# One slot between the turn of the attention weights and their product with the values, from tile 2 on

## The chip, the cores and the metric

The kernel runs on one core of a Trainium2 chip. The metric is the device time of one execution in microseconds, as a median of several runs. The core has five engines that run side by side, each through its own list of instructions in order: TensorE (matmul), VectorE, ScalarE, GpSimd and SyncE. They wait for one another through semaphores. Transfers between the main memory (HBM) and the on-chip memories run on 16 DMA engines; here SyncE issues the ordinary ones and GpSimd the gathers. TensorE writes its results to banks of a small memory (PSUM), from which VectorE and ScalarE read.

## The reference, cut to what matters

The program is one step of a one-layer decoder over 1024 prompt tokens and 32 sample tokens (8 sequences of 4, with 512 cached tokens each), width 1024, all in float32:

```python
x = x + concat(diff_attention(rmsnorm(x) @ W_in), pool_mixer(...)) @ W_out   # 4 heads, 4 pooling groups
x = x + peer(rmsnorm(x))            # 8 heads x 16 chosen experts a token, out of 16384
x = x + sigmoid(rmsnorm(x) @ W_gate) * (p @ W_ple)
y = rmsnorm(x)
# attention of one head: a = softmax(q1 k1 + bias) - lam * softmax(q2 k2 + bias);  out = a @ v
# peer: for each token and head, gather 16 rows u and 16 rows v from the tables;
#       out += sum_k gate_k * gelu(xn . u_k) * v_k
```

## The kernel before, in words

The prompt is cut into 8 tiles of 128 tokens. The peer part sets the beat of the whole program. For each tile and peer head, 16 rows of the joined table (a row of u and a row of v, 8 KB together) are gathered for each of the 128 tokens. One gather fetches one such row for all 128 tokens. The ring `uv_rows` holds 8 gathers. A *slot* is the work for two gathers; a peer head has 8 slots and a tile 64. There are 528 slots with the samples, numbered s = 0, 1, ..., and 19 more before them with negative numbers, which hold the first work of the program.

In slot s the engines do this. GpSimd (`fetch`) issues two gathers, each when the adds that used its place in the ring are done, so it fetches the rows of slot s + 4 when those of slot s have been added. VectorE (`dot`) takes the dot products of two gathered rows with the tokens, and after them a step of the choice of experts for a later peer head (`choose_part`). ScalarE (`weigh`) applies the gelu to the dots and writes two scaled diagonals, `diag`. TensorE (`add_rows`, lines 974 and 976) multiplies the diagonals by the v halves and so adds them to two banks. In every eighth slot (s = 2 modulo 8) TensorE also computes the scores of the experts for a later head (`route`, line 949).

All other work is laid over these slots. The order of each engine's instructions is written out by slot numbers: in every slot, each engine runs `front_step(s)`, which asks for each piece whether it belongs to s. TensorE runs it before `add_rows` of the same slot, ScalarE after `weigh`, VectorE after the dots and the step of the choice. Slots 0 to 63 project the tiles. Attention for tiles 0 and 1 is done before slot 0 and for tiles 2 to 7 in slots 67 to 189. Then the samples' attention follows, and from slot 322 the gates. `ATT[t]` holds the slots of a tile t:

- `turn`, `band`, `pool`: q and k are turned (line 553), then the pooling products (lines 589 and 591, then 601).
- `scores`: for each of the 4 heads the scores in one or two chunks (line 617). VectorE adds bias and takes the maxima (line 1532), and ScalarE takes the exponentials (line 1193), one slot later (`late`).
- `keys`: VectorE combines the two softmaxes to the weights of a head (line 1550).
- `weights`: TensorE turns the weights of a head to banks TA and TB (line 629), and ScalarE copies them to on-chip memory (`keep_weights`, lines 1203 and 1208).
- `values`: TensorE multiplies the turned weights by the values (line 648). Before it, it waits until the copy has emptied the banks. After the last head ScalarE copies the sums (`keep_values`).
- `norm`, `heads`, `out`: the norm over each head, the turn of the heads (line 553; VectorE copies it in the next slot, line 1584), and two halves of the output product, each 8 matmuls of 128x512 (line 671), which VectorE adds to x in the next slot (line 1592). SyncE loads and stores x around it.

The start of each tile from 2 on is a number written out in `attention_slots` (67, 84, 101, 123, 145, 167). Before the change, `values` from tile 2 on are the same slots as `weights`; for tiles 0 and 1 they are one slot later. `norm`, `heads` and `out` are reckoned from the last of them, `end`. In `front_step` of TensorE the pieces of one slot come in this order: for each tile turn, band, pool, heads, scores, output; then weights, then values. `BACK_FREE`, and from it every slot of the samples (`C0`, `C_PAGE`, `C_SCORES`, `C_VALUES`, `C_OUT`, `C_END`), is reckoned from the last output slot of tile 7. The gate jobs' slots are numbers written out.

Of the kernel before, what the change touches and what calls it, by code (L numbers as in the profile page):

```python
# [87 lines left out]
Attention = namedtuple("Attention", "load load_s1 turn band pool chunks scores keys weights values norm heads out")  # L88


def attention_slots(t):

    if t < EARLY:
        b = -LEAD + (1, 4)[t]
        first = -LEAD + (2, 6)[t]
        scores = [[first + h] for h in range(H)]
        weights = [first + 2 + h for h in range(H)]
        values = [first + 3 + h for h in range(H)]
        end = values[-1]
        return Attention(None, None, b, b + 1, b + 2, [(0, (t + 1) * T)], scores, weights, weights, values,  # L100
                         (end + 1, end + 1), end + 2, (end + 3, end + 4))
    b = {2: 67, 3: 84, 4: 101, 5: 123, 6: 145, 7: 167}[t]
    W = (t + 1) * T
    if W <= 512:
        chunks = [(0, W)]
        scores = [[b + 3 + 2 * h] for h in range(H)]
    else:
        cut = min(512, W - NEAR)
        chunks = [(0, cut), (cut, W)]
        scores = [[b + 3 + 3 * h, b + 4 + 3 * h] for h in range(H)]  # L110
    keys = [s[-1] + 2 for s in scores]
    weights = [s[-1] + 3 for s in scores]
    end = weights[-1]
    if t == EARLY:
        load = load_s1 = W_IN_FREE
    else:
        load, load_s1 = (ATT[t - 1].weights[h] + 1 for h in (H - 2, H - 1))
    return Attention(load, load_s1, b, b + 1, b + 2, chunks, scores, keys, weights, weights, (end + 1, end + 2), end + 3,
                     (end + 5, end + 6))


# [1 line left out]
for t in range(NT):  # L123
    ATT.append(attention_slots(t))
# [2330 lines left out]
```

## Time and profile before

| what | value |
|---|---|
| time, median of 3 runs | 3189.36 us (3188.24 to 3190.01) |
| the profiled execution, its own time | 3185.96 us |
| its span on the core | 3184.0 us |
| TensorE, VectorE, ScalarE, GpSimd busy | 74%, 70%, 30%, 41% |
| moved by DMA | 1266.57 MB, mean 398 GB/s over the span |
| slots with two gathers each | 528 (1056 gathers) |

The busy time of an engine says how much of the span it works. The profile's rows also name what an engine waited for: an arrow in brackets gives the idle time before an instruction and the engine and line that released it. The table of stretches shows the transfer rate beside the busy times, and the clock that TensorE was granted as a share of 2.4 GHz.

### The profile page before, as it was taken

To read this page: it belongs to the slowest core of one execution; us is meant where nothing else is said; L and a number is where in the kernel's file an instruction comes from. 1 tells how busy PE (TensorE), PEld (TensorE's weight loads), DVE (VectorE), ACT (ScalarE), POOL (GpSimd) and SP (SyncE) were. 2 spreads that over 40 slices of the span, in tenths; PEclk is the share of its full clock that TensorE was granted. 3 is DMA by queue.
4 is the path that set the end of the run, shared out by engine and by line. 5 is a ranking of instruction groups with operands and counts; after the bars stand their busy time and mean duration, and the time that the engine had idled before them with its cause. 6 is when DMAs were issued, how large, how long until landed. Compare 5 with 4: busy or idle time off the path is not lost.

```text
span 3184.0 us, 53323 instructions
## 1 busy us (share of the span) xinstructions
PE 2356.8 (74%) x20876; PEld 934.7 (29%) x20876; DVE 2234.2 (70%) x5466; ACT 950.0 (30%) x2427; POOL 1314.7 (41%) x1143
## 2 busy tenths in 40 slices
PE   8879999668777778757876667576777676677656
PEld 3543334223333333313432222122222222222112
DVE  1366667768778688756667666577777777777775
ACT  2212232234335354312322122123332322223222
POOL 0024433433334343435654543344444444444442
PEclk9999999878989889867788887788888897888778
DMA  6579999999999999999999999999999999999996
GB/s 264 179 284 420 421 413 417 417 416 395 416 417 409 407 416 416 412 409 418 417 416 411 417 416 410 414 410 416 407 414 417 420 407 421 408 420 410 420 416 281
DMA packets 202899, 1266.57 MB, mean 398 GB/s; under 512 B 24144, under 2 KB 27496, under 8 KB 60944
## 3 DMA queue, kind: packets, MB, share of 16 engines
q0 software_dynamic: 159808, 1133.76, 86.8%
q1 hardware_dynamic: 41404, 129.11, 10.2%
q8 instruction: 164, 2.69, 0.3%
q14 instruction: 87, 0.71, 0.1%
q10 hardware_dynamic: 1436, 0.29, 0.0%
HBM read 1234.61 MB, written 28.65 MB: 397 GB/s over the span
## 4 chain that ended last, share of the span: by engine, by line
DMA 31%; PE 14%; DVE 6%; POOL 3%; issue 3%; DVEq 2%; ACT 2%; POOLq 0%; ACTq 0%
DMA ring<-in_uv,idx 31%; PE sc L974 7%; DVE ring L1831 3%; POOL ring L2045 3%; PE sc L1007 2%; PE route L949 1%; DVEq L1841 1%; PE sc L976 1%; ACT diag L1367 1%; ACT hgelu L1362 0%; PE sc L873 0%; DVE x L1880 0%; PE sc L967 0%; PE sc L843 0%; POOL front L2061 0%
## 5 line engine op out<-in xcount | busy, mean ns | idle before, releaser
L2045 POOL DMA_INDIRECT ring<-in_uv,idx x1056 | 1235.2, 1170 | 1661.1 <-PE sc L976 1421.9
L974 PE MATMUL sc<-ring,diag 32*32 32x512 f32 x8192 | 1246.1, 728 | 667.6 <-ACT diag L1367 617.8
L1831 DVE CUSTOM_DVE_ANT_0 ring<-ring,xn_cur 128x1024 f32<-128x1024 f32 x1056 | 1280.2, 1221 | 652.8 <-DMA ring<-in_uv,idx 647.3
L976 PE MATMUL sc<-ring,diag 32*32 32x512 f32 x8192 | 1246.1, 728 | 0.0
L974 PEld LDWEIGHTS sc<-ring,diag 32*32 32x32 f32 x8192 | 273.1, 118 | 1456.0 <-ACT diag L1367 1033.1
L1362 ACT ACTIVATE hgelu<-hdot 128x2 f32<-128x2 f32 x528 | 107.5, 204 | 1816.4 <-DVE hdot L1831 1816.0
L1367 ACT ACTIVATE diag<-gate_d,hgelu 128x32 f32<-128x32 f32 x1056 | 281.8, 314 | 21.2
L976 PEld LDWEIGHTS sc<-ring,diag 32*32 32x32 f32 x8192 | 272.3, 118 | 2.3 <-issue 2.3
L531 PE MATMUL sc<-big,front 128*128 128x512 f32 x448 | 209.4, 612 | 3.6 <-DVE front L1477 3.5
L1362 ACT ACT_TABLE_LOAD x128 | 164.2, 1283 | 2.2
L949 PE MATMUL route<-big,xnT 128*128 128x256 f32 x560 | 135.3, 396 | 0.0
L949 PEld LDWEIGHTS route<-big,xnT 128*128 128x128 f32 x560 | 107.3, 197 | 52.3 <-issue 38.3
L949 PE MATMUL route<-front,xnT 128*128 128x256 f32 x464 | 111.9, 396 | 13.4 <-DMA front<-wqk_scratch 12.6
L531 PEld LDWEIGHTS sc<-big,front 128*128 128x128 f32 x448 | 83.0, 193 | 125.3 <-issue 124.8
L1007 PE MATMUL sc<-front 128*128 128x512 f32 x256 | 118.0, 604 | 0.0
L949 PEld LDWEIGHTS route<-front,xnT 128*128 128x128 f32 x464 | 88.9, 197 | 53.5 <-issue 27.9
L671 PE MATMUL sc<-big,front 128*128 128x512 f32 x192 | 87.2, 607 | 0.0
L1831 DVE DVE_READ_ACCUMULATOR2_ANT hdot<- 128x1 f32 x1056 | 86.5, 82 | 0.0
L648 PE MATMUL work<-big,front 128*128 128x128 f32 x264 | 41.1, 312 | 58.4 <-ACT front L1208 24.2
L1355 ACT ACT_TABLE_LOAD x65 | 83.4, 1283 | 1.1
L1007 PEld LDWEIGHTS sc<-front 128*128 128x128 f32 x256 | 46.3, 189 | 69.6 <-issue 69.4
L1193 ACT ACTIVATE front<-front 128x384 f32<-128x384 f32 (+5 forms) x48 | 41.9, 874 | 54.8 <-DVE front L1532 54.8
(296 smaller groups left out, 2311.0 us busy)
## 6 DMA issues: line engine op xcount, KB each, us to landing
front<-wqk_scratch SPq DMA_DIRECT2D x27, 1024.0 KB
ring<-in_uv,idx POOLq DMA_INDIRECT x1056
big<-in_w_in SPq DMA_DIRECT2D x8, 1024.0 KB, 14.3
wqk_scratch<-front SPq DMA_DIRECT2D x8, 1024.0 KB, 6.8
big<-wqk_scratch SPq DMA_DIRECT2D x8, 1024.0 KB, 22.5
x<-x_scratch SPq DMA_DIRECT2D x12, 512.0 KB, 8.9
front<-in_x SPq DMA_DIRECT2D x8, 512.0 KB, 8.2
xnT<-in_wq_t POOLq DMA_DIRECT2D x8, 512.0 KB, 4.4
```

The costliest lines, as they stand in the source:

```text
L531: mm = pe.matmul(bank[b], xTp[t % 2][:, k, :], w_in_sb[:, k, at:at + W4], start=(k == 0), stop=(k == KD - 1))
L671: mm = pe.matmul(bank[b], a.xT[:, k, :], a.wo[:, k, c * W4:(c + 1) * W4], start=(k == 0), stop=(k == KD - 1))
L949: mm = pe.matmul(bank[RT][:, 0:256], xnT[:, k, :], w[:, k * 256:(k + 1) * 256], start=(k == 0), stop=(k == KD - 1))
L974: pe.matmul(sc[own, 0, :], diag[own, r, :], uv_rows[own, r, D:D + W4], start=opens_sum, stop=closes).then_inc(row_added[r], 1)
L976: pe.matmul(sc[other, 1, :], diag[own, r, :], uv_rows[own, r, D + W4:2 * D], start=opens_sum, stop=closes).then_inc(row_added[r], 1)
L1007: mm = pe.matmul(bank[b], x2T[:, k, :], wg_sb[:, k, c * W4:(c + 1) * W4], start=(k == 0), stop=(k == KD - 1))
L1193: act.activation(rows, rows, ACT.Exp, bias=st[:, NMAX + col:NMAX + col + 1], accum_out=st[:, LSUM + col:LSUM + col + 1]).then_inc(s_exp, 1)
L1355: act.activation(ex[:, n % GATES, :], top2[:, :], ACT.Exp, bias=gst[:, NTOP + n % 2:NTOP + n % 2 + 1], accum_out=es[:, n % GATES:n % GATES ...
L1362: act.activation(hgelu[:, n % 2, at], hdot[:, n % 2, at], ACT.Gelu).then_inc(gelu_done, 1)
L1367: act.activation(diag[:, (n * TOPK + j) % RING, :], gate_d[:, n % 2, j, :], ACT.Copy, scale=hgelu[:, n % 2, j:j + 1]).then_inc(diag_ready, 1)
L1831: dve.tensor_tensor_reduce(uv_rows[:, k % RING, 0:D], uv_rows[:, k % RING, 0:D], xn_cur[:, :], 1.0, 0.0, ALU.mult, ALU.add, hdot[:, n % 2, ...
L2045: pool.indirect_dma_start(uv_rows[:, k % RING, :], None, uv, bass.IndirectOffsetOnAxis(ap=idx[:, n % PH, j:j + 1], axis=0)).then_inc(row_i ...
```

## The change

From tile 2 on, the slots of the value products are those of the weights plus one. `end`, from which norm, heads and output are reckoned, is the last of the new slots. In numbers, for tile 3: the weights stay in 90, 92, 94, 96; the values go from these to 91, 93, 95, 97; the norm from 97, 98 to 98, 99; the heads from 99 to 100; the output from 101, 102 to 102, 103. Tile 4 starts in slot 101 as before. `BACK_FREE` goes from 190 to 191, and all slots of the samples and of the gate weights' loads go with it. Tile 3 gets its load of q, k and u as before, since that is reckoned from the weights.

```diff
         scores = [[b + 3 + 3 * h, b + 4 + 3 * h] for h in range(H)]
     keys = [s[-1] + 2 for s in scores]
     weights = [s[-1] + 3 for s in scores]
-    end = weights[-1]
+    values = [w + 1 for w in weights]
+    end = values[-1]
     if t == EARLY:
         load = load_s1 = W_IN_FREE
     else:
         load, load_s1 = (ATT[t - 1].weights[h] + 1 for h in (H - 2, H - 1))
-    return Attention(load, load_s1, b, b + 1, b + 2, chunks, scores, keys, weights, weights, (end + 1, end + 2), end + 3,
+    return Attention(load, load_s1, b, b + 1, b + 2, chunks, scores, keys, weights, values, (end + 1, end + 2), end + 3,
                      (end + 5, end + 6))
```

## Rows read from the trace of the kernel before

**Rows 1.** The page's first part: busy us (share) x instructions by engine.
```profile
PE 2356.8 (74%) x20876; PEld 934.7 (29%) x20876; DVE 2234.2 (70%) x5466; ACT 950.0 (30%) x2427; POOL 1314.7 (41%) x1143
```

**Rows 2.** Stretches: width, busy by engine, TensorE's clock, DMA share, GB/s.
```profile
240.00:440.00 200.00, 187.68 (x1427) 72.79 (x1433) 135.52 (x332) 58.35 (x150) 79.69 (x69) 0.98 1.02 421
600.00:1330.00 730.00, 551.70 (x5128) 240.93 (x5132) 573.57 (x1400) 307.32 (x709) 283.13 (x245) 0.88 1.01 412
772.00:778.00 6.00, 6.00 (x64) 1.63 (x48) 5.46 (x14) 3.67 (x7) 2.74 (x3) 0.76 0.85 307
996.00:1002.00 6.00, 6.00 (x84) 2.02 (x69) 5.68 (x16) 4.21 (x9) 4.75 (x5) 1.00 1.00 382
1122.00:1128.00 6.00, 6.00 (x64) 3.56 (x48) 5.82 (x14) 3.88 (x8) 3.87 (x4) 1.00 1.00 382
1296.00:1305.00 9.00, 6.85 (x84) 1.98 (x69) 8.54 (x23) 4.67 (x12) 6.08 (x6) 0.81 0.97 348
730.00:741.00 11.00, 11.00 (x153) 4.58 (x153) 9.21 (x21) 5.27 (x12) 5.89 (x6) 1.00 0.85 317
832.00:840.00 8.00, 8.00 (x113) 3.06 (x112) 7.40 (x22) 3.64 (x12) 4.58 (x5) 1.00 1.01 382
954.00:966.00 12.00, 10.83 (x139) 4.88 (x128) 8.55 (x19) 6.19 (x13) 9.06 (x7) 1.00 0.96 357
1080.00:1088.00 8.00, 8.00 (x70) 5.88 (x69) 7.15 (x17) 1.71 (x5) 2.68 (x2) 1.00 0.82 304
1210.00:1214.50 4.50, 4.50 (x60) 2.99 (x55) 3.28 (x13) 1.22 (x4) 3.32 (x3) 1.00 0.94 346
```

**Rows 3.** Stretches for line 974's instructions alone (half of a slot's adds).
```profile
720.30:722.30 2.00, 1.94 (x16) 0.46 (x16) 1.00 1.02 426
770.60:774.30 3.70, 3.66 (x16) 0.64 (x16) 0.50 0.94 385
```

**Rows 4.** Line 648, value products: idle us before them and times, by releaser.
```profile
  ACT front L1203: 62.1, 25
```

**Rows 5.** Timeline of ScalarE in slot 92: start, us, instruction, idle before.
```profile
762.63 0.53 ACT L1367 ACTIVATE diag<-gate_d,hgelu 128x32 f32<-128x32 f32 x2
...
766.58 0.72 ACT L1193 ACTIVATE front<-front 128x512 f32<-128x512 f32 x1 [2.12 <-DVE front L1532]
...
768.00 0.57 ACT L1203 ACTIVATE front<-turn 128x512 f32<-128x512 f32 x1
```

**Rows 6.** Timeline of TensorE, pieces of slots 84, 85, 86, 145 and 146.
```profile
711.41 8.12 PE L671 MATMUL sc<-big,front 128*128 128x512 f32 x16
719.37 1.04 PE L553 MATMUL turn<-ident,front 128*128 128x128 f32 x8
...
729.18 0.38 PE L589 MATMUL work<-front 128*128 128x128 f32 x2
...
730.74 0.39 PE L591 MATMUL work<-front 128*128 128x128 f32 x2
...
732.93 1.16 PE L601 MATMUL work<-front 128*128 128x128 f32 x8
...
1073.18 7.13 PE L671 MATMUL sc<-big,front 128*128 128x512 f32 x16
...
1082.99 3.72 PE L949 MATMUL route<-front,xnT 128*128 128x256 f32 x16
```

**Rows 7.** Timeline: VectorE's last choice instruction of slot 84, ScalarE's diagonals of slot 144.
```profile
715.27 0.42 DVE L1790 FIND_INDEX8 ind<-top,sc_sb 128x8 uint32<-128x256 f32 x1
...
1066.21 0.53 ACT L1367 ACTIVATE diag<-gate_d,hgelu 128x32 f32<-128x32 f32 x2
```

**Rows 8.** Timeline of GpSimd: first fetch behind the adds of slots 85, 86, 146.
```profile
732.67 0.93 POOL L2045 DMA_INDIRECT ring<-in_uv,idx  x1 [8.05 <-PE sc L976]
...
735.63 1.20 POOL L2045 DMA_INDIRECT ring<-in_uv,idx  x1 [0.79 <-PE sc L976]
...
1090.04 0.94 POOL L2045 DMA_INDIRECT ring<-in_uv,idx  x1 [4.33 <-PE sc L976]
```

## Prediction

> **What bounds the kernel now.** I read the page's table of engines first. TensorE is the busiest, and it is busy for 74% of the span [rows 1], so no compute engine fills the time. The second view was the busy time by stretch, for its last column, the bytes that the DMA engines moved. From 240 to 440 us, where no attention tile runs, they move 421 GB/s. From 600 to 1330 us, which holds all that the change touches except the step for the samples, they move 412 GB/s [rows 2]. So the kernel is bound by its transfers, nearly all of them gathered expert rows. Over 730 us the stretch loses 730 x (1 - 412/421) = 15.6 us against the full rate. That is the most that a better order of work here can win, and any order that lets the transfers run dry costs its whole dry time.
>
> The same view, cut finely, says where the 15.6 us go. With lost time = width x (1 - rate/421), four dips follow a weights-and-values slot: 1.6 us (772 to 778), 0.6 (996 to 1002), 0.6 (1122 to 1128) and 1.6 (1296 to 1305), together 4.3 us. Five dips lie where a tile ends and the next begins: 2.7 (730 to 741), 0.7 (832 to 840), 1.8 (954 to 966), 2.2 (1080 to 1088) and 0.8 (1210 to 1214.5), together 8.3 us [rows 2]. The remaining 3 us are too small and scattered to place.
>
> How a dip comes about: the ring holds eight gathered rows, two for each slot, so GpSimd may fetch the rows of slot s + 4 only when TensorE has added those of slot s. Two rows are 2 x 128 x 8192 bytes = 2.1 MB, 5.0 us at 421 GB/s. The adds of a slot take TensorE 1.9 us, twice that at half clock [rows 3]. So TensorE has about 3 us of each slot free for the front, and the ring forgives some 10 us of delay. Beyond that the DMA engines stop.
>
> **What the change removes.** In slot s TensorE turned a head's weights, waited until ScalarE had copied them, multiplied by the values, and only then added slot s's rows. The waits for the first copy come to 62.1 us over 25 waits [rows 4]. They cost time only where the ring ran out. The plainest is slot 92. The diagonals for the adds were ready at 762.63 + 0.53 = 763.2, but ScalarE then waited for VectorE's maxima of the next head's scores until 766.58, and its copy of the weights started at 768.00 [rows 5]. The adds came at 770.6, at half clock [rows 3]. After the change they start at 763.2, some 7 us earlier, and the dip at 772 should go. In slot 183 (tile 7, last head) the adds move ahead of 2.0 us of products and a shorter wait, about 3 us, and most of the dip at 1296 goes. The two small ones go too. No product is removed: each now stands ahead of the next slot's adds, where its wait is mostly over. Bounds: nothing won, or all 4.3 us. I take 4.0. The first product of tile 2 also waits for the stored values on a DMA, but there the transfers are the old values and output weights themselves, no dip follows, and I count nothing.
>
> **What the change moves.** The end of each tile is reckoned from the last values slot, so the copy of the values, norm, turning of heads, both output products and the storing of x1 go one slot later, while the next tile's start is written out and stays. Everything from BACK_FREE on (expert weights, samples, gate weights) also goes one slot later; the gate jobs stay. The pieces on TensorE: an output product is 7.13 us (8.12 partly at half clock), the turn of q and k 1.04, the band products 730.74 + 0.39 - 729.18 = 1.95 (eight rows, first and last shown), pool 1.16, a route 3.72 [rows 6]. Now boundary by boundary, each reckoned forward with these pieces and 1.9 us of adds per slot.
>
> Tiles 2 to 3, slots 84, 85, 86. Before: output half 0 and turn; half 1 and band; pool. After: turn; half 0 and band; half 1 and pool. Here a new wait appears. The turn needs the bank that the heads leave, and VectorE now frees it in the same slot 84, after that slot's dots and choice step, which ends at 715.27 + 0.42 = 715.7 [rows 7], plus about 0.7 for its own copy: 716.4. Behind the turn queue slot 84's adds, and for them GpSimd waits. TensorE reaches slot 84 at 711.41 and used to fill that time with an output product [rows 6]; now it idles 5 us. Then: turn to 717.4, adds to 719.3; half 0 and band 9.1, adds to 730.3; half 1 and pool 8.3, adds to 740.5. Before, the fetches behind the last two came at 732.67 and 735.63 [rows 8]. The first is 2.4 us earlier, the second 4.9 us later. The transfers ran dry at about 730 before; with the rows of one slot added they run dry at 735.3 and wait to 740.5, 5.2 us against 2.7. Stores that move with the product fill up to 1.2 of that. So it costs 1.3 to 2.5 more, and I take 2.0. Tiles 3 to 4 have the same pattern and a smaller dip before (0.7): also 2.0.
>
> Tiles 4 to 5: a route stood with half 0 in slot 122; after, that slot has the route alone, and the burst spreads better: -0.5. Tiles 5 to 6 are the reverse. Slot 144 loses half 0, so its adds start when the diagonals are ready, at 1066.21 + 0.53 = 1066.7 [rows 7], and end at 1068.6. Slot 145: half 0 and turn 8.2, adds to 1078.7. Slot 146 holds a route already: 3.7 + 7.1 + 1.95 = 12.8, adds to 1093.4, where the fetch came at 1090.04 [rows 8]. That leaves 14.7 us with no new gather. The backlog is 1.7 (dry at about 1080.5 before), the new rows 5.0 and other traffic about 2, so some 6 us are lost against 2.2. I take +3.3, bounds 2 and 6. Tiles 6 to 7: +0.7. The sum is 2.0 + 2.0 - 0.5 + 3.3 + 0.7 = +7.5, with bounds 3 and 12.
>
> The sample phase moves by one slot, which lays its value products on some route slots. Its rates before are much those of the stretch above, so I take 0, plus or minus 2. The gate weights' loads are issued one slot later too, well ahead of the first gate job in slot 322, so I expect no wait there, and the end of the program is untouched.
>
> **Sum.** -4.0 + 7.5 + 0 = +3.5 us. The profiled execution took 3185.96 us (span 3184.0), so its like would take 3189.5. The median of the runs shown is 3189.36, 3.4 above that execution, so I forecast 3192.9 for the median.
>
> Weighed against the trace: after the 5.9 us of idle in slot 92 the granted clock is 0.50, the lower of TensorE's two levels, and sixteen of the add matmuls' records take 3.66 us of busy time instead of 1.94 [rows 3]. The Trainium skill, "TensorE: Matmul & The Clock Gate", section "HAM oscillation — how this bites in real kernels", says that gaps in the array's work throttle it and the work after them starts cold. By that rule the change helps where it closes gaps and hurts where it opens one (slot 84). The trace agrees with the rule in slot 92. It is a rival below.
>
> The Trainium skill's "Perfetto Trace Analysis", section "Roofline", puts a single core's ceiling at about 435 GB/s. By it the stretch would have 730 x (1 - 412/435) = 38.6 us to win, not 15.6. No stretch read here holds that rate, and the measured 421 decides.
>
> **The rivals.** A difference of under 0.2% (6.4 us) cannot be told from none for this kernel.
> - Forecast: gains and losses nearly cancel, 3192.9, own range 3187 to 3196. For it: no dip is deep, and both kinds are short. Chance 0.60.
> - Slower: output product, band and route stack up at the boundaries. Slot 146 and the two slots 84 and 101 with the idle of the turn cost their upper bounds, 12 us, and the values give back only 2: 3189.4 + 10 = 3199.4. It decides from the point where TensorE is over 10 us behind with two such slots in a row. For it: the pieces are measured. Against: the same burst cost only 0.7 us from tile 3 to 4. Chance 0.24.
> - Faster by removal alone: the boundaries cost what they did, the values dips go and so do the scattered 3 us: 3189.4 - 7.3 = 3182.1. Against it is the reckoning of slots 84 and 146. Chance 0.06.
> - The clock: with fewer waits TensorE stays at 2.4 GHz (the stretch has a mean of 0.88 now) and all dips shrink by more than half: 3189.4 - 10 = 3179. Chance 0.03.
> - Nothing moves: the front's lateness is hidden as before, 3189.4, half a microsecond either way. Chance 0.07.
>
> Range for 8 in 10: 3184 to 3201. Faster 0.08 (the two faster rivals, less what falls within 6.4 us), slower 0.25 (the slower rival and the forecast's tail), same 0.67.
>
> **What would show it.** In the changed profile: waits of the value products for the copy fall well under 62 us; the dip at 772 is gone; the adds of slot 92 follow the diagonals at once; TensorE idles before the turn of tile 3's q and k, waiting for VectorE; the dips at tile ends are deeper, the one after tile 5's above all; and the rate over the stretch stays within 2 GB/s of 412. If the five dips at tile ends sum to less than 8.3 us, the step on the boundaries is wrong. If the four others stay, the step on the removal is.

## Result: 0.26% slower

| | before | after |
|---|---|---|
| median, us | 3190.03 (3188.24 to 3196.36, 10 runs) | 3198.77 (3194.44 to 3201.66, 10 runs) |
| profiled execution, its span | 3185.96, 3184.0 | 3196.89, 3194.9 |
| mean granted clock | 0.862 | 0.866 |
| time of slots 64 to 190 | 750.3 | 759.7 |

The ratio is 1.0026, interval 1.0018 to 1.0034. So the loss is small but clear of the noise. The range of the prediction (3184 to 3201) holds the time. Its likeliest case (3192.9, own range 3187 to 3196) does not: the slower rival (3199.4) came out, which had a chance of 0.24.

The last row is the distance between the gelus of slots 64 and 190. It holds the attention of tiles 2 to 7, and it is the measure used below. Timeline of ScalarE, these two instructions, before and then after:

```profile
577.92 0.20 ACT L1362 ACTIVATE hgelu<-hdot 128x2 f32<-128x2 f32 x1 [5.69 <-DVE hdot L1831]
...
1328.22 0.20 ACT L1362 ACTIVATE hgelu<-hdot 128x2 f32<-128x2 f32 x1 [2.75 <-DVE hdot L1831]
```

```profile
578.82 0.20 ACT L1363 ACTIVATE hgelu<-hdot 128x2 f32<-128x2 f32 x1 [5.69 <-DVE hdot L1832]
...
1338.54 0.20 ACT L1363 ACTIVATE hgelu<-hdot 128x2 f32<-128x2 f32 x1 [3.52 <-DVE hdot L1832]
```

So 9.4 of the 10.9 us between the two profiled executions lie in this stage. The added line moves every line number after it up by one.

### The profile page after: what moved, and what is told of

Its sections match the earlier page's. It is cut to its first block, busy times and chain, and to the rows that moved or that the text cites. A ratio compares the mean times of both kernels' runs of the same rounds, so it can differ in the third digit from the quotient of the medians.

```text
span 3194.9 us, 53324 instructions
## 1 busy us (share of the span) xinstructions
PE 2364.9 (74%) x20876; PEld 941.8 (29%) x20876; DVE 2234.1 (70%) x5466; ACT 951.4 (30%) x2428; POOL 1309.2 (41%) x1143
## 3 DMA queue, kind: packets, MB, share of 16 engines
q1 hardware_dynamic: 41404, 129.11, 10.2%
## 4 chain that ended last, share of the span: by engine, by line
DMA 29%; PE 15%; DVE 8%; issue 3%; POOL 2%; ACT 2%; DVEq 2%; another core or an unknown queue 0%; POOLq 0%; ACTq 0%
DMA ring<-in_uv,idx 29%; PE sc L975 7%; DVE ring L1832 4%; PE sc L1008 2%; POOL ring L2046 2%; PE sc L977 1%; PE route L950 1%; ACT diag L1368 1%; DVEq L1842 1%; POOL front L2062 0%; PE sc L844 0%; PE sc L968 0%; ACT hgelu L1363 0%; PE sc L672 0%; PE sc L874 0%
## 5 line engine op out<-in xcount | busy, mean ns | idle before, releaser
L950 PEld LDWEIGHTS route<-big,xnT 128*128 128x128 f32 x560 | 109.0, 200 | 54.4 <-issue 40.2
L950 PEld LDWEIGHTS route<-front,xnT 128*128 128x128 f32 x464 | 89.9, 199 | 53.3 <-issue 27.9
L968 PE MATMUL sc<-ring,diag 128*32 128x512 f32 x64 | 35.3, 683 | 26.3 <-ACT diag L1368 19.4
```

Source lines behind the costliest of these rows:

```text
L950: mm = pe.matmul(bank[RT][:, 0:256], xnT[:, k, :], w[:, k * 256:(k + 1) * 256], start=(k == 0), stop=(k == KD - 1))
```

## The profile after

The page's first part, as in [rows 1], does not tell the two kernels apart: TensorE is busy for 2364.9 us instead of 2356.8, VectorE for 2234.1 instead of 2234.2. The stretches do. Columns as in [rows 2]:

```profile
600.00:1340.00 740.00, 553.91 (x5130) 237.10 (x5115) 572.63 (x1398) 306.36 (x709) 276.07 (x246) 0.87 0.99 405
745.00:836.00 91.00, 62.81 (x607) 27.74 (x601) 75.55 (x192) 39.57 (x89) 32.81 (x30) 0.89 1.02 419
730.00:745.00 15.00, 15.00 (x130) 6.46 (x136) 7.73 (x16) 4.62 (x12) 4.52 (x4) 1.00 0.68 246
836.00:856.00 20.00, 20.00 (x180) 9.45 (x165) 13.26 (x36) 6.36 (x18) 7.33 (x8) 1.00 0.75 274
1088.00:1102.00 14.00, 14.00 (x97) 8.06 (x103) 6.33 (x18) 1.96 (x7) 2.54 (x3) 1.00 0.62 238
1225.00:1237.00 12.00, 12.00 (x117) 7.64 (x115) 9.94 (x24) 2.93 (x9) 4.01 (x4) 1.00 0.75 277
```

The full rate (240 to 440 us) is 421 GB/s again. The stretch as a whole falls from 412 to 405 GB/s. The second row spans all of tile 3 between two ends, and it moves 419: no dip is left behind its weights-and-values slots. The four rows under it are the ends of tiles 2, 3, 5 and 6. By width x (1 - rate/421) they lose 6.2, 7.0, 6.1 and 4.1 us. The end of tile 4 (966 to 976, 401 GB/s) loses 0.5.

From here on "dry time" is this loss, added up over the dips in slots 64 to 190, that is over runs of 1 us steps with under 400 GB/s. Lone steps that fall only a little short are left out. With every step under 400 counted, each kernel has 3 to 6 us more (18.5 before and 27.5 after), so a difference of less than 1 us in these sums means nothing. At the five tile ends the dry time is 8.3 us before and 24.0 after. Between them ("mid-tile") it is 5.0 before and 0.1 after. The sum grows by 10.8 us, the stage by 9.4.

What makes the first end deep is seen around the turn of q and k in slot 84. VectorE, TensorE and GpSimd in their timelines:

```profile
715.82 0.73 DVE L1585 TENSOR_SCALAR front<-turn,front 128x512 f32<-128x512 f32 x1
...
716.70 1.94 PE L554 MATMUL turn<-ident,front 128*128 128x128 f32 x8 [4.42 <-DVE front L1585]
...
721.55 0.94 POOL L2046 DMA_INDIRECT ring<-in_uv,idx  x1 [7.82 <-PE sc L977]
...
732.10 1.44 POOL L2046 DMA_INDIRECT ring<-in_uv,idx  x1 [8.37 <-PE sc L977]
...
741.93 1.21 POOL L2046 DMA_INDIRECT ring<-in_uv,idx  x1 [7.15 <-PE sc L977]
```

And the stretches of TensorE's turn (first row) and of half of slot 84's adds (second), each for that line alone:

```profile
716.60:718.70 2.10, 1.94 (x8) 1.56 (x8) 0.50 1.03 429
```

```profile
718.50:722.00 3.50, 3.14 (x16) 0.64 (x16) 0.63 1.02 417
```

TensorE idles 4.42 us for the bank of the heads. After that idle time the granted clock is 0.50 in the turn and 0.63 in the adds. The turn takes 1.94 us instead of 1.04 [rows 6], the adds 3.14 instead of 1.94 [rows 3]. Then come two slots with an output product each, and the fetch behind the third (741.93) starts 20.4 us after the one behind the first.

There is a second way in which a late output product costs time, and the forecast did not have it. VectorE adds each half to x in the next slot (line 1592, now 1593), and the dots of the slot behind that stand after it in VectorE's list. In slot 87:

```profile
739.61 0.69 DVE L1593 TENSOR_TENSOR front<-sc,front 128x512 f32<-128x512 f32 x1 [6.60 <-PE sc L672]
...
741.11 1.22 DVE L1832 CUSTOM_DVE_ANT_0 ring<-ring,xn_cur 128x1024 f32<-128x1024 f32 x1
```

VectorE waits 6.60 us for the product. The dots behind it then start without a wait, so their rows were there: at this end it is the product that held them, not the dry transfers. VectorE's waits for the product and for gathered rows in slots 64 to 190 (idle us, times, longest), before and after:

```profile
DVE ring L1831 <- DMA ring<-in_uv,idx: 104.0, 83, 3.3
DVE front L1592 <- PE sc L671: 10.0, 6, 3.0
```

```profile
DVE ring L1832 <- DMA ring<-in_uv,idx: 101.6, 71, 3.8
DVE front L1593 <- PE sc L672: 27.9, 5, 6.9
```

The waits for the product grow by 17.9 us, at the same tile ends as the dips. The waits for rows do not grow, although the transfers are dry for 10.8 us more. Other waits of VectorE shrink, and in all it is idle for 172.3 us of the stage instead of 161.6.

## The experiments

Theories. *Boundary*: the norm, the heads and the output of a tile, called its tail here, moved one slot onto the next tile's start; they cost the time. *Values*: the products of weights and values one slot later cost or win it. *Samples*: the phase behind BACK_FREE costs it. Later a fourth came: dry time moves from place to place within the stage.

| kernel | slots 64 to 190 | dry at tile ends | dry mid-tile | VectorE's wait for the output product | ratio to before (interval) |
|---|---|---|---|---|---|
| before | 750.3 | 8.3 | 5.0 | 10.0 | |
| before_again | 750.4 | 9.1 | 5.2 | 10.8 | |
| after | 759.7 | 24.0 | 0.1 | 27.9 | 1.0026 (1.0018 to 1.0034) |
| after_again | 756.7 | 20.4 | 0.1 | 24.4 | |
| e1_values_only | 750.2 | 13.5 | 0.2 | 17.2 | 0.9999 (0.9990 to 1.0008) |
| e1_again | 750.2 | 14.0 | 0.2 | 17.9 | |
| e2_tail_only | 759.4 | 18.4 | 4.4 | 23.3 | 1.0030 (1.0019 to 1.0040) |
| e3_tails_2_3_kept | 752.4 | 15.7 | 0.2 | 15.7 | 1.0002 (0.9993 to 1.0011) |
| e4_samples_only | 752.5 | 10.7 | 6.7 | 10.2 | 0.9990 (0.9981 to 0.9999) |
| e5_tail_5_kept | 756.8 | 21.0 | 0.2 | 23.8 | 1.0023 (1.0014 to 1.0032) |
| e6_heads_sooner | 759.0 | 23.3 | 0.2 | 24.0 | 1.0026 (1.0015 to 1.0038) |
| e7_output_in_parts | 749.9 | 4.3 | 10.0 | 1.1 | 0.9993 (0.9984 to 1.0002) |
| e7_again | 747.3 | 4.1 | 7.4 | 1.1 | |
| e9_both | 749.3 | 10.9 | 3.1 | 6.0 | 0.9996 (0.9987 to 1.0005) |

The names with "again" are a second profile of the same program. In all 14 profiles the stage less both dry times is 735 to 737 us. That is bookkeeping and not yet a cause: the same bytes at 421 GB/s take the same time, and what is left over is called dry. The stages behind it differ little: 759.3 to 764.6 us for slots 190 to 320, 1072.6 to 1075 for slots 320 to 527.

**e1_values_only.** The change, with the tail left where it was:

```diff
     values = [w + 1 for w in weights]
-    end = values[-1]
+    end = weights[-1]
```

> The value products one slot later, but end is reckoned from the weights, so the output products, the norm and the samples stay in their slots of before. Boundary theory (the loss comes from output products pushed onto the next tile's first pieces; the values' shift itself gains): the dips at 772, 996, 1122 and 1296 us go, the five at tile ends stay at about 8 us, and the kernel takes 4 us less than before, 3186 where before takes 3190. Rival, values theory (the products in the next slot collide with the next scores and cost by themselves): 3195 or more, as in the changed kernel. Rival, samples theory (the slot that the samples and gate loads lose costs): same as the boundary theory here.

Median 3188.58 us against 3188.74. There is no loss, so the shift of the values does not cause it. But the gain forecast for it is missing too. The stretch from 600 to 1330 us moves 411 GB/s where it was 412 [rows 2]. The end of tile 4 (949 to 967, 306 GB/s) loses 4.9 us, where the two profiles of before lose 1.8 and 5.4. Mid-tile dry time fell from 5.0 to 0.2 us, and at the tile ends it rose from 8.3 to 13.5 (14.0 against 9.1 in the second profiles). Norm, heads and output keep their slots there; only the values of the last head and their copy come one slot later, into the slot of the norm. TensorE's waits in 600 to 1330 us, before and in this kernel (idle us, times, longest):

```profile
PEld sc L974 <- ACT diag L1367: 167.2, 99, 6.8
PE sc L974 <- ACT diag L1367: 108.2, 41, 5.9
PEld work L648 <- ACT front L1203: 42.2, 18, 6.2
PE work L648 <- ACT front L1208: 24.2, 16, 3.5
PE work L648 <- ACT front L1203: 19.8, 7, 5.9
```

```profile
PEld sc L975 <- ACT diag L1368: 219.9, 132, 6.5
PE sc L975 <- ACT diag L1368: 151.8, 59, 6.3
PEld work L649 <- ACT front L1204: 15.2, 6, 4.9
PE work L649 <- ACT front L1204: 7.9, 4, 4.0
...
PE work L649 <- ACT front L1209: 1.5, 2, 0.8
```

The waits for the copied weights did shrink, from 86.2 to 24.6 us. The waits for the diagonals took their place, from 275.4 to 371.7 us. (The sums hold waits of matmuls and of weight loads, which can overlap.) TensorE is mostly earlier at points where it then waits for ScalarE.

Slot 92, the plainest case of the prediction, shows why. VectorE's first dot, ScalarE's diagonals and the first of TensorE's adds of slot 93, before (the diagonals of slot 92 stand at 762.63 [rows 5]):

```profile
766.46 1.21 DVE L1831 CUSTOM_DVE_ANT_0 ring<-ring,xn_cur 128x1024 f32<-128x1024 f32 x1
...
770.12 0.53 ACT L1367 ACTIVATE diag<-gate_d,hgelu 128x32 f32<-128x32 f32 x2
...
775.59 0.61 PE L974 MATMUL sc<-ring,diag 32*32 32x512 f32 x1
```

The same in this kernel, with slot 92's diagonals and the first of its adds ahead:

```profile
762.53 0.53 ACT L1368 ACTIVATE diag<-gate_d,hgelu 128x32 f32<-128x32 f32 x2
...
762.90 0.61 PE L975 MATMUL sc<-ring,diag 32*32 32x512 f32 x1 [1.47 <-ACT diag L1368]
...
766.36 1.22 DVE L1832 CUSTOM_DVE_ANT_0 ring<-ring,xn_cur 128x1024 f32<-128x1024 f32 x1
...
770.03 0.53 ACT L1368 ACTIVATE diag<-gate_d,hgelu 128x32 f32<-128x32 f32 x2
...
770.40 1.06 PE L975 MATMUL sc<-ring,diag 32*32 32x512 f32 x1
```

The diagonals of slot 92 come within 0.1 us of each other in the two profiles, so their times can be compared here. Slot 92's adds start 7.7 us sooner (762.9 against 770.6 [rows 3]), and slot 93's adds 5.2 us sooner (770.4 against 775.6). But slot 93's diagonals follow slot 92's after 7.5 us in both. They don't depend on those adds: their dots stand on VectorE behind the bias and maxima of the next head's scores, without a gap, and on ScalarE behind the exponentials and the copy [rows 5]. TensorE's adds stay ahead until slot 96 (786.5 against 789.6), and in slot 97 the kernel before has caught up (791.4, here 791.5). Nor does VectorE wait longer for rows with the dip at 772 than without it: its waits for gathered rows in slots 88 to 101 come to 3.8 us before (3.1 in the second profile) and to 2.7 here (3.5).

**e2_tail_only.** Before, with the tail one slot later and the values where they were:

```diff
-    end = weights[-1]
+    end = weights[-1] + 1
```

> The value products stay with the weights, but end is one later, so norm, heads, output and samples move as in the changed kernel. Boundary theory: the dips at tile ends sum to some 23 us instead of 8, and the values' dips of 4 us stay, so 3190 + 14.5 = 3204, slower than the changed kernel. Values theory: no loss, 3190. Samples theory: slower than before by the whole 9 us, 3199, with the dips at tile ends as before.

Median 3198.14 us: the tail alone gives the whole loss of the change, by the ratios as by the stage (759.4 against 759.7). It stopped 6 us short of the boundary theory's number: mid-tile dips stay (4.4 us), but the ends are shallower than in the changed kernel. The ends of tiles 2 and 3:

```profile
729.00:744.00 15.00, 15.00 (x140) 6.05 (x134) 7.84 (x18) 5.20 (x12) 5.27 (x5) 1.00 0.69 247
837.00:855.00 18.00, 18.00 (x152) 8.54 (x145) 11.31 (x32) 5.44 (x14) 7.71 (x7) 1.00 0.80 290
```

They lose 6.2 and 5.6 us, the other three 6.5 together where they lose 10.8 in the changed kernel. What the tail adds at the ends is 18.4 - 8.3 = 10.1 us. e1 adds 13.5 - 8.3 = 5.2 there. With both, 8.3 + 10.1 + 5.2 = 23.6 us, and the changed kernel has 24.0, but 20.4 in its second profile. End by end the two do not add up (table below): at tile 4's end they would make 4.8 us, and the changed kernel has 0.6.

**e3_tails_2_3_kept.** The changed kernel, with the tails of tiles 2 and 3 back in their places:

```diff
-    end = values[-1]
+    end = weights[-1] if t in (2, 3) else values[-1]
```

> As the changed kernel, but the ends of tiles 2 and 3 are in their slots of before. Boundary theory: of the 14.5 us of new dry time, the 9.8 us of the first two boundaries (6.2 + 7.0 after against 2.7 + 0.7 before) go: 3199 - 9.8 = 3189. Samples theory: 3199 unchanged. Values theory: 3199 unchanged.

Median 3188.37 us, ratio 1.0002. The loss is gone. Its stretches at the ends of tiles 2, 3 and 5:

```profile
730.00:742.00 12.00, 12.00 (x158) 4.92 (x156) 10.24 (x22) 5.26 (x12) 6.47 (x7) 1.00 0.85 313
833.00:842.00 9.00, 9.00 (x128) 3.84 (x120) 7.63 (x22) 3.95 (x12) 6.20 (x6) 1.00 0.92 340
1079.00:1095.00 16.00, 16.00 (x118) 9.06 (x116) 8.14 (x19) 1.96 (x7) 3.69 (x5) 1.00 0.69 261
```

The first two lose 3.1 and 1.7 us instead of 6.2 and 7.0. The third still loses 6.1. The stage is 7.3 us shorter than in the changed kernel (4.3 than in its second profile), and the two dips account for 8.4. The ends of tiles 5 and 6 keep the changed kernel's dips; the dry time missing mid-tile sets off most of that, 15.9 us in all against 13.3 before.

**e4_samples_only.** Before, with the samples and the gate weights' loads one slot later:

```diff
-BACK_FREE = ATT[-1].out[1] + 1
+BACK_FREE = ATT[-1].out[1] + 2
```

> The kernel before with all slots of the samples and of the gate weights' loads one later. Boundary theory: 3190, within 2 us. Samples theory: the loss is here, 3195 to 3199.

Median 3187.12 us, ratio 0.9990: the samples theory falls. The forecast's 0, plus or minus 2, holds for that term (the interval, 0.9981 to 0.9999, even lies just below 1). This kernel also shows how far the stage scatters by itself: nothing in slots 64 to 190 is edited, and its profile has 752.5 us and 17.4 us of dry time there, where the two of before have 750.3 and 750.4, 13.3 and 14.3.

**e5_tail_5_kept.** The changed kernel, with the tail of tile 5 back, so that slot 146 has no output product with its route:

```diff
-    end = values[-1]
+    end = weights[-1] if t == 5 else values[-1]
```

> As the changed kernel, but the end of tile 5 is in its slots of before, so its second output product (slot 145) does not share slot 146 with the route. Boundary theory: the dip after tile 5 goes from 6.0 back to about 2.2 us, the others stay: 3199 - 3.8 = 3195. Rival, each boundary's loss is made up by the next (the ring only moves it): 3199 unchanged.

Median 3195.27 us, ratio 1.0023. Its stretch behind tile 5:

```profile
1088.00:1100.00 12.00, 12.00 (x136) 7.23 (x136) 8.67 (x20) 3.21 (x12) 4.58 (x5) 1.00 0.88 324
```

12 x (1 - 324/421) = 2.8 us instead of 6.0. The stack of route and output product is a place of loss of the size forecast, and the dip is 5.8 in the changed kernel's second profile too. What it is worth in time is not shown. The stage takes 756.8 us, and the changed kernel's two profiles have 759.7 and 756.7. The median was expected at 3195, but its ratio is 1.0023 against 1.0026, and the two intervals overlap.

**e6_heads_sooner.** The changed kernel with the norm of both pairs in one slot and the heads one slot sooner, the output products left late. The new wait of the turn goes, the stack stays:

```diff
-    return Attention(load, load_s1, b, b + 1, b + 2, chunks, scores, keys, weights, values, (end + 1, end + 2), end + 3,
+    return Attention(load, load_s1, b, b + 1, b + 2, chunks, scores, keys, weights, values, (end + 1, end + 1), end + 2,
                      (end + 5, end + 6))
```

> As the changed kernel, but the norm's two steps stand in one slot (end + 1) and the turn of the heads in end + 2, so that the bank is free before the next tile's turn; the output products stay in the changed kernel's slots. Theory that the turn's new wait for VectorE matters (TensorE idle 4 to 5 us in slots 84 and 101 and then at half clock): two thirds of the growth at the first two boundaries go, 3199 - 6 = 3193. Rival, only the stacking of both output products with band and pool matters: slots 84 and 101 have nothing else to do, so 3199 unchanged, or slower by what the norm's wait on ScalarE costs VectorE.

Median 3195.55 us, ratio 1.0026. The turn of slot 84:

```profile
712.62 1.41 PE L554 MATMUL turn<-ident,front 128*128 128x128 f32 x8
```

The turn starts some 4 us sooner. The first two ends lose 2.6 us (736 to 742, 262 GB/s, and the steps ahead of it) and 3.8 us (832 to 848, 319 GB/s) instead of 6.2 and 7.0: in place, the wait and the low clock behind it are about half of those dips. But the next three lose 4.3, 7.1 and 5.5 instead of 0.6, 6.0 and 4.2, and the sum is 23.3 against 24.0. The edit moves norm and heads at all of these ends, so it is not shown whether the later dips come from it or from the time won at the first two. The expected 3193 is not reached: by the ratio the kernel is as slow as the changed one, and the rival expectation, that only the stacking matters, holds for the time.

**e7_output_in_parts.** This tests the other direction. Before, with each output half in two parts of 4 matmuls, spread over 3 slots for tiles 2 and 3 and over 4 slots for tiles 4 to 6:

```diff
+    o = a.out[0]
+    if t < EARLY or t == NT - 1:
+        parts = [(a.out[c], c, p) for c in range(2) for p in range(2)]
+    elif t < 4:
+        parts = [(o, 0, 0), (o + 1, 0, 1), (o + 1, 1, 0), (o + 2, 1, 1)]
+    else:
+        parts = [(o, 0, 0), (o + 1, 0, 1), (o + 2, 1, 0), (o + 3, 1, 1)]
...
-                for k in range(KD):
+                for k in range(4 * part, 4 * part + 4):
```

> The kernel before with each output product of tiles 2 to 6 cut into two parts of 4 matmuls, laid over three slots for tiles 2 and 3 and four slots for tiles 4 to 6; values, norm, heads and samples as before. Boundary theory (what counts is TensorE's work in neighbouring slots against the ring's 10 us): the five dips at tile ends shrink from 8.3 to some 2 us: 3189 - 6 = 3183. Rival, the dips come from waits and not from the sum of the work: 3189 unchanged, and the second half's adding on VectorE, one slot nearer to the next scores, costs 1 or 2 us.

Median 3187.12 us, ratio 0.9993: a miss. The ends shrink to 4.3 us. But the dip in the middle of tile 3 deepens, where no instruction was edited. The stretch of that dip:

```profile
778.00:789.00 11.00, 7.71 (x80) 3.42 (x64) 10.48 (x25) 8.26 (x17) 3.81 (x4) 0.81 0.69 240
```

It loses 4.7 us, and 4.2 in the second profile (773 to 785, 273 GB/s), where before lost 1.6 in that place [rows 2]. VectorE sees the same from its side. Its wait for the output product falls from 10.0 to 1.1 us, and its wait for gathered rows rises from 104.0 to 109.0.

**e9_both.** The changed kernel with e7's parts, the values of the last head back in their slot, and with them the tail, so that both kinds of dips are taken on at once (e7's lines not shown again):

```diff
-    values = [w + 1 for w in weights]
-    end = values[-1]
+    values = [w + 1 for w in weights[:-1]] + weights[-1:]
+    end = weights[-1]
```

> The kernel before with both cures: the value products of the first three heads of each tile from 2 on one slot later (the last head's stay with its weights, so the norm and all that follows keep their slots), and the output products of tiles 2 to 6 in parts as in the kernel with parts alone. Each cure alone left the stage from slot 64 to 190 at 750 us: with the values later the mid-tile dry time went from 5.0 to 0.2 us and that at tile ends rose from 8.3 to 13.5; with parts the tile ends went from 8.3 to 4.3 and the mid-tile rose from 5.0 to 10.0. Additive theory (the rises were one execution's luck): 0 plus 4, the stage takes 741 us, the kernel 3188 - 9 = 3179. Rival, the dry time moves to wherever TensorE has least room, and only its sum counts: 748 to 750 us, 3187. Between them: what is left is only the last heads and tile ends, 745, 3183.

Median 3187.94 us, ratio 0.9996. The two removals do not add up to a gain. Dry time is 14.0 us in all, 10.9 of it at the ends. The rival expectation, that only the sum of dry time counts and that it moves, gave 3187; the interval of the ratio leaves out the 3179 and 3183 of the others.

**before_again, after_again, e1_again, e7_again.** One execution each, to see how far a profile repeats.

> The kernel before once more, for a second profile of the same program. If the place and depth of the dips are the program's, they agree with the first profile within 1 us each; if TensorE's clock level at the start of a burst moves them, the dips at tile ends differ by 1 to 3 us each while their places stay.

> The changed kernel once more, a second profile: dry time at tile ends 24 us within 3, mid-tile 0 to 1, slots 64 to 190 in 760 us. If it is luck, 15 to 20.

> The kernel with the values alone one slot later, a second profile. If the gain moves to the tile ends by a mechanism, these are 12 to 15 us again; if the first look was luck, 8 to 9, and the stage takes 745.

> The kernel before with the output products in parts, a second profile. If the gain moves to the middle of the tiles by a mechanism, these dips are 8 to 10 us again; if luck, 5.

They took 3186.77, 3194.23, 3190.21 and 3187.47 us. Sums of dry time repeat to 1 us for before and e1, to 3 or 4 us for the others. Single dips repeat less well. Stretches of the first profile of before (first fence) and of the second:

```profile
925.00:945.00 20.00, 16.66 (x129) 7.77 (x130) 14.09 (x39) 2.75 (x11) 6.84 (x6) 1.00 1.02 419
```

```profile
925.00:945.00 20.00, 17.39 (x95) 7.96 (x96) 13.18 (x37) 2.75 (x11) 6.00 (x4) 0.74 1.02 419
948.00:967.00 19.00, 19.00 (x180) 8.65 (x178) 12.32 (x30) 7.90 (x18) 8.79 (x8) 1.00 0.82 302
```

One program, but a granted clock of 1.00 in one and 0.74 in the other. At the lower clock slot 121's adds took 3.7 us instead of 1.9 and the route of slot 122 took 4.7 instead of 3.7. The adds of slot 122 ended 3.1 us later, and the dip behind tile 4 lost 5.4 us instead of 1.8.

## Why the prediction was right and wrong

**Place: right.** The dips at tile ends grew, the others went. TensorE idled before the turn for VectorE's copy, which ended at 715.82 + 0.73 = 716.55 (forecast 716.4). e2 and e3 show that the moved tail is the cause, e1 and e4 that the values and the samples are not. The mechanism, stacking on TensorE, is right as far as it goes. It went by one path only, from late adds over late fetches to dry transfers, and left out VectorE's wait for the output product, which grew by 17.9 us.

**The removal: the step that failed.** Forecast -4.0 us. As dry time that was right: mid-tile it fell by 4.9 us. As time it is nothing: e1 does this alone and its stage takes 750.2 us in both profiles, against 750.3 and 750.4. A gain of 4 us lies outside the interval of its ratio (0.9990 to 1.0008). The step was that in slot 92 "they start at 763.2, some 7 us earlier, and the dip at 772 should go", and then all four dips were booked as time won. The adds do start earlier (762.9 in e1), and so do those of the next four slots. But the diagonals of slot 93 do not come sooner: VectorE and ScalarE, not TensorE, set when they come, and VectorE waited for rows there no longer with the dip than without. And the tile ends are deeper by 5.2 us.

**The boundaries: a term mis-sized by less than it seems.** Forecast +7.5 us. In the changed kernel the ends grew by 15.7 us, in its second profile by 12.1. Part of that may be the 5.2 that e1 shows at the ends without any moved tail. The tail alone (e2) adds 10.1, inside the bounds 3 to 12. End by end, in us of dry time:

| end of tile | before | forecast | tail alone (e2) | values alone (e1) | after | after_again |
|---|---|---|---|---|---|---|
| 2 | 2.8 | 4.7 | 6.3 | 2.3 | 6.2 | 5.6 |
| 3 | 0.7 | 2.7 | 5.5 | 2.3 | 7.0 | 6.6 |
| 4 | 1.8 | 1.3 | 1.6 | 5.0 | 0.6 | 0.4 |
| 5 | 2.3 | 5.5 | 3.6 | 1.8 | 6.0 | 5.8 |
| 6 | 0.8 | 1.5 | 1.3 | 2.2 | 4.2 | 1.9 |

The tail's own excess is at the ends of tiles 2 and 3. Two things were wrong there. First, the turn and the adds of slot 84 were priced at full clock, 1.0 and 1.9 us, although the forecast itself opened an idle gap of 5 us ahead of them and weighed the low clock as a rival of the opposite sign only. They ran at 0.50 and 0.63, and the fetches behind slots 84 to 86 came at 721.55, 732.10 and 741.93, where the adds were forecast to end at 719.3, 730.3 and 740.5. The same happened in slot 101, where the turn also took 1.94 us in e2. Second, tile 3's end was never reckoned forward. It was given the 2.0 of tile 2's by likeness. GpSimd's fetches behind slots 101 and 103, before and after:

```profile
822.99 1.02 POOL L2045 DMA_INDIRECT ring<-in_uv,idx  x1 [7.11 <-PE sc L976]
...
836.67 1.41 POOL L2045 DMA_INDIRECT ring<-in_uv,idx  x1 [0.79 <-PE sc L976]
```

```profile
825.38 1.06 POOL L2046 DMA_INDIRECT ring<-in_uv,idx  x1 [6.00 <-PE sc L977]
...
846.95 1.21 POOL L2046 DMA_INDIRECT ring<-in_uv,idx  x1 [7.31 <-PE sc L977]
```

The two slots took 13.7 us before and 21.6 after, for rows worth 10 us. (A slot of the stage takes 750.3 / 126 = 6.0 us on average and not 5.0: of the 300 MB moved from 600 to 1330 us, 258 are gathered rows.) That is 7.9 us more, and the dip grew by 6.3; this end lost almost all that was added to it. The small dip before (0.7) was read as room, and little was left. The slower rival had nearly the right total by adding 12 us at the ends and taking off 2; the ends grew by 12.1 and 15.7. It gave the removal 2 us where e1 gives none, and the tail 12 where e2 gives 10.1, so its 3199.4 is in part two errors that cancel. It put the 12 us in slots 84, 101 and 146. e3 bears that out for tiles 2 and 3. In its place for tile 5, though, the plain forecast was right:

```profile
1086.15 3.72 PE L950 MATMUL route<-front,xnT 128*128 128x256 f32 x16
1089.71 7.03 PE L672 MATMUL sc<-big,front 128*128 128x512 f32 x16
...
1100.07 0.94 POOL L2046 DMA_INDIRECT ring<-in_uv,idx  x1 [10.79 <-PE sc L977]
```

Slot 146 has the pieces as summed. From slot 144's diagonals to the end of slot 146's adds it is 27.2 us (from 1072.62 + 0.53 to 1100.4), forecast 26.7.

The Trainium skill, "TensorE: Matmul & The Clock Gate", section "HAM oscillation — how this bites in real kernels", says that work behind a gap in the array's activity starts throttled. The trace agrees in slot 84: clock 0.50 behind 4.42 us of idle time. Where no such gap stands (slot 146), the clock is 1.00 in the stretch from 1088 to 1102.

**The sum.** Forecast -4.0 + 7.5 = +3.5 us. By the kernels that do one part each it is 750.2 - 750.3 = -0.1 for the values and 759.4 - 750.3 = +9.1 for the tail, 9.0 together, and the changed kernel's stage is 9.4 us longer (6.4 in its second profile). Of the 5.9 us missing in the forecast, 3.9 are the removal's and 1.6 the boundaries'; the other 0.4 is left open, and a second profile can move any of these by up to 3 us.

**What stays open.** Counted in dry time every profile closes: the stage is 735 to 737 us and its dry time. Why an edit changes the sum or only moves it is not explained by that. Moving all tails (after, e2) raises it by 6 to 11 us. Taking dips away mid-tile (e1), at the ends (e7) or at both (e9) leaves it within 3 us of before. In e6 the first two dips retreat and the later three give it back. In slot 93 of e1 VectorE and ScalarE hold the pace where TensorE and the transfers had been freed. My reading is that this holds for the whole middle of a tile, so that a dip taken away there leaves the ring fuller but TensorE no nearer to the next tile's end. That is argued, not shown: no kernel here lightens VectorE or ScalarE in these slots or changes the depth of the ring. It would not explain e7, where the ends were eased and mid-tile dips grew. Nor is it shown how the 9 us of the tail divide between the two paths, VectorE's wait for the product and the late fetches: no kernel here moves VectorE's add to a later slot than the product. In the changed kernel the waits for the product grew and those for rows did not, which speaks for the first. That e7 took the first away (10.0 to 1.1 us) without gaining time shows that in the kernel before it was not a wait whose removal pays.

**From the profiled execution to the median** the forecast added 3.4 us; in the changed kernel it is 3198.77 - 3196.89 = 1.9.

## What to carry to other kernels

Price a moved piece by what it stacks on at the place where it arrives, each place reckoned forward by itself, with the clock that the gap ahead of it will leave. Before a wait taken from one engine is booked as time, look at what the next step of the loop needs from the others. Follow every reader of the moved result, not only the queue behind it: here VectorE stood waiting for the product. A boundary that shows hardly any loss may be one that is nearly full. And take a dip away alone before you count it as won: here 5 us of dry time vanished mid-tile and as much appeared at the tile ends, and only a kernel with that one edit showed it.

## What was not expected of the hardware

The same program shows a granted clock of 1.00 in one execution and 0.74 in another over the same 20 us (925 to 945 us, above), and one dip behind it differs by 3.6 us, while the whole differs by 0.8 us (3185.96 and 3186.77). A single dip of one profile is therefore no measure of an edit of this size, and the sums over the stage repeat better, though only to 3 or 4 us in some kernels.
